# Two moves in the written-out order of a decoder trunk: the last tile's gate transposes, and one strip's low parts

## The reference

```python
for i in range(DEPTH):                                   # 2
    h = rms_norm(x, norm_mix_pre[i])
    proj = h @ w_in[i]                                   # 1024 x 2944
    y_a = gmlp_mixer(...)                                # 4 heads
    y_b = retention_mixer(...)                           # 6 heads
    y_c = swa_sink_mixer(...)                            # 6 heads, window 128, softmax with sinks
    mix = jnp.concatenate([y_a, y_b, y_c], axis=-1) @ w_out[i]
    x = x + rms_norm(mix, norm_mix_post[i])
    h = rms_norm(x, norm_ffn_pre[i])
    gate, up = split_cols(h @ w_ffn_in[i], (D_FF, D_FF)) # 2816 each
    f = (jax.nn.silu(gate) * up) @ w_ffn_out[i]
    x = x + rms_norm(f, norm_ffn_post[i])
    ple = rms_norm(p[i] @ w_ple_proj[i], ple_norm[i])    # 256 -> 1024
    x = x + jax.nn.sigmoid(x @ w_ple_gate[i]) * ple      # 1024 -> 1024
```

## Time and profile before

| | |
|---|---|
| median of 3 runs | 1223.09 us (1222.53 to 1223.4) |
| the profiled execution | 1222.93 us |
| its span, first to last instruction | 1221.2 us |
| TensorE busy | 1213.1 us, 7753 matmuls |
| VectorE, ScalarE, GpSimd busy | 843.1, 620.3, 175.6 us |
| mean granted TensorE clock | 1.000 |
| DMA | 126.36 MB, mean 103 GB/s |

### The profile page before, as it was taken

How to read it: one execution, slowest core, us unless ns; L and a number is a source line. 1 busy time by engine, 2 the same in 40 slices (tenths; PEclk the granted TensorE clock), 3 DMA queues, 4 the chain that set the end, 5 groups by cost and what they waited for, 6 DMA issues and landing times.

```text
span 1221.2 us, 20253 instructions
## 1 busy us (share of the span) xinstructions
PE 1213.1 (99%) x7753; PEld 1094.4 (90%) x7753; DVE 843.1 (69%) x1321; ACT 620.3 (51%) x1218; POOL 175.6 (14%) x260
## 2 busy tenths in 40 slices
PE   9999999999999999999999999999999999999998
PEld 7887988999999988888898879889999999888887
DVE  5665646888888843367977656468988887433788
ACT  7544426455555533347674643364655555322474
POOL 3044621000000000013030547120000000000120
PEclk9999999999999999999999999999999999999999
DMA  8332232233333354310344222331333333534001
GB/s 294 109 112 66 70 104 71 69 106 106 108 107 109 108 173 156 128 62 18 104 140 119 73 83 69 94 96 53 107 105 109 107 99 116 164 146 172 18 18 69
DMA packets 129135, 126.36 MB, mean 103 GB/s; under 512 B 5840, under 2 KB 111440, under 8 KB 129040
## 3 DMA queue, kind: packets, MB, share of 16 engines
q1 hardware_dynamic: 128352, 124.55, 32.7%
q10 hardware_dynamic: 688, 0.53, 0.2%
HBM read 120.99 MB, written 2.10 MB: 101 GB/s over the span
## 4 chain that ended last, share of the span: by engine, by line
PE 95%; DVE 3%; ACT 2%; issue 1%; POOL 0%; DVEq 0%; ACTq 0%
PE bank L1044 30%; PE bank L1046 29%; PE bank L1045 29%; PE bank L1275 2%; DVE w_lo L1978 1%; ACT prob L1739 1%; PE bank L1392 1%; PE bank L1332 1%; PE bank L1353 1%; PE bank L1376 1%; PE bank L1340 0%; PE bank L1388 0%; PE bank L1397 0%; DVE prob L2353 0%; PE bank L1285 0%
## 5 line engine op out<-in xcount | busy, mean ns | idle before, releaser
L1044 PE MATMUL bank<-h_hi,w_hi 128*128 128x256 f32 (+2 forms) x672 | 200.6, 298 | 0.1
L1046 PE MATMUL bank<-h_hi,w_lo 128*128 128x256 f32 (+2 forms) x672 | 199.9, 298 | 0.0
L1045 PE MATMUL bank<-h_lo,w_hi 128*128 128x256 f32 (+2 forms) x672 | 199.9, 297 | 0.0
L1976 DVE TENSOR_TENSOR w_lo<-raw,w_hi 128x1024 fp32r<-128x1024 f32 x70 | 83.2, 1226 | 133.7 <-ACT w_hi L1470 133.4
L1044 PE MATMUL bank<-w_hi,h_hi 128*128 128x384 f32 (+2 forms) x436 | 156.9, 360 | 0.8 <-DVE w_lo L1978 0.7
L1470 ACT ACTIVATE w_hi<-raw 128x1024 fp32r<-128x1024 f32 x70 | 70.6, 1053 | 160.6 <-PE bank L1046 160.6
L1045 PE MATMUL bank<-w_lo,h_hi 128*128 128x384 f32 (+2 forms) x436 | 151.8, 348 | 0.0
L1046 PE MATMUL bank<-w_hi,mid_lo 128*128 128x512 f32 x352 | 137.0, 389 | 0.0
L1044 PEld LDWEIGHTS bank<-h_hi,w_hi 128*128 128x128 f32 x672 | 128.6, 191 | 4.1 <-issue 0.5
L1046 PEld LDWEIGHTS bank<-h_hi,w_lo 128*128 128x128 f32 x672 | 128.6, 191 | 3.5
L1045 PEld LDWEIGHTS bank<-h_lo,w_hi 128*128 128x128 f32 x672 | 128.6, 191 | 3.4
(11 more groups left out here) (293 smaller groups left out, 2918.1 us busy)
## 6 DMA issues: line engine op xcount, KB each, us to landing
raw<-in_w_ffn_in SPq DMA_DIRECT2D x88, 512.0 KB, 3.8
raw<-in_w_ffn_out SPq DMA_DIRECT2D x44, 512.0 KB, 4.3
raw<-in_w_in SPq DMA_DIRECT2D x22, 512.0 KB, 5.3
raw<-in_w_in SPq DMA_DIRECT2D x24, 384.0 KB, 3.4
raw<-in_w_out SPq DMA_DIRECT2D x16, 512.0 KB, 3.8
gw<-in_w_gate SPq DMA_DIRECT2D x16, 512.0 KB, 3.7
raw<-in_w_ple SPq DMA_DIRECT2D x4, 512.0 KB, 5.9
x<-in_x_in SPq DMA_DIRECT2D x3, 512.0 KB, 6.9
```

The source lines that it names most:

```text
L1044: pe.matmul(out_ap, a_hi, b_hi, start=start, stop=False, skip_group_check=True)
L1045: pe.matmul(out_ap, a_hi, b_lo, start=False, stop=False, skip_group_check=True)
L1046: return pe.matmul(out_ap, a_lo, b_hi, start=False, stop=stop, skip_group_check=True)
L1976: last = dve.tensor_tensor(lo, raw[q % RAWS][:, cols], hi, ALU.subtract)
```

## The change

Two edits in `plan_schedule`, both in each of the two layers. After strip `("in", "bk", 1)` the one entry `conv` of strip a0 becomes two, `hi` at the same place and `lo` behind the entries of the next unit. And the entry `("T", "gate", 3)` moves behind `("mm", ple, 2)`.

```diff
     for layer in range(depth):
         at = plan_mixers()
         u = 4
+        late = None
         for s in ins[1:]:
             for m in range(TILES):
                 if u >= 6:
                     mm(s, m)
                 for e in at.pop(u, ()):
                     add(*e)
+                if late is not None:
+                    add("lo", late)
+                    late = None
                 u += 1
-            close(s)
+            if s == ("in", "bk", 1):
+                late = SIDX[s] + SLOTS
+                add("hi", late)
+            else:
+                close(s)
         mm(o[0], 0)
...
         mm(ple, 1)
         add("post", "ple", 0)
+        mm(ple, 2)
         add("T", "gate", 3)
-        mm(ple, 2)
         add("gsum", "S1")
         add("post", "ple", 1)
         add("gsum", "S3")
```

## The result

The changed kernel takes 1228.36 us (median of 5 runs, 1227.69 to 1228.58), the kernel before 1222.69 us beside it (5 runs, 1222.53 to 1223.4): 1.0044 times as long, interval 1.0033 to 1.0054. Forecast were 1226.4 us. The direction was right and the size was not: +5.7 us against +3.5, and 0.8 us above the upper end of the range.

A forecast was written before the change was run, and what follows sets the result against it. TensorE was taken to bound the kernel. From 1222.93 us, moving a0's low parts gave −2.0 us and moving the transposes 2 × 2.73 = +5.5, so 1226.4 us; the range was 1224.1 to 1227.6.

The forecast's parts named there:

- What bounds the kernel: Whole span: TensorE, busy 1213.1 of 1221.2 us, sets the time; moved instructions count only by changing its standstills.
- the start and ScalarE's side: Softmax of tile 2: swa_prev starts about 82.65, 3.7 us earlier; ScalarE's exponentials about 86.9, 2.1 us earlier.
- The spare 1.1 us: Softmax transposes: prob ready at 91.5, 1.1 us before TensorE wants it, covering a w_lo a quarter slower.
- signs of being wrong: Listed: a remaining wait for prob, a gate product under 2.5 us later, GpSimd's tile 1 addition at 0.2 us.
- the rule named in the prediction: VectorE and GpSimd: whichever takes the shared pair first holds it all instruction; applied to GpSimd's small addition, deciding 1.06 us.
- two pieces: Around side-projection tile 3: the 2.73 us per layer shows as TensorE waits, about 2.1 on h_lo, 1.0 on ple_n.
- (e): Side-projection tile 3: the new waits lower TensorE's clock, at most 1.7 us more a layer, 1229.8 us; chance 0.02.
- the second wait: Before the first gate product: TensorE waits 1.0 us for ple_n instead of 0.5.
- (a): GpSimd's small addition before ple_n starts first in both layers, moved transposes cost 1.67 us a layer: 1224.2 us; chance 0.08.
- (b): Later in the layer, short TensorE stops give back at most 0.5 us a layer: 1225.4 us; chance 0.06.
- (c): First gate product does not hang on the moved transposes; ple_n comes early, the 0.5 stop goes: 1219.9 us; chance 0.03.
- (d): Moving w_lo gains nothing, as beside GpSimd's rotations it ends over 1.1 us later than reckoned: 1228.4 us; chance 0.05.

The follow-up runs named there:

- low_only: Kernel before with only the low parts of strip a0 moved behind swa_prev, transposes left in place: 1222.64 us, 0.9997 of the kernel before.
- low_hold: Kernel before with a0's low parts moved, and GpSimd's rotation of tile 2 held until prob of that tile is normalised: 1220.66 us, 0.9981.
- hold_only: Kernel before with neither move, only GpSimd's rotation of tile 2 held until prob of that tile is normalised: 1223.65 us, 1.0005.
- trans_fill: Kernel before with only the transposes moved, plus eight unread matmuls behind them filling TensorE's stop: 1228.47 us, 1.0045.
- trans_post: Kernel before with the transposes moved, and side-projection tile 1's norm ahead of their copies and sum S1 on ScalarE and VectorE: 1227.27 us, 1.0037.
- trans_only: Kernel before with only the transposes moved behind side-projection tile 3 of 4, a0's low parts left in place: 1228.56 us, 1.0045.
- full_hold: Changed kernel with GpSimd's rotation of tile 2 held until prob of that tile is normalised: 1226.22 us, 1.0029 of the kernel before.
- full_hold_fill: Changed kernel with GpSimd's rotation of tile 2 held and eight unread matmuls filling TensorE's stop behind the transposes: 1225.88 us, 1.0026 of the kernel before.

## Why the prediction was right and wrong

**What bounds the kernel: right.** Every microsecond of the change is a stop of TensorE or a slower step of it.

**Edit 1, the start and ScalarE's side: right** to 0.1 us. **The gain, and the step that failed.** It is the sentence "I take 1.0, since 1.1 us of spare time cover a `w_lo` that is a quarter slower", which rests on "the four run in 4.2 us as before". The term of the sum was −2.0 us, and −0.4 came. `prob` came 1.9 us later than worked out: 0.75 from the small instruction, 0.8 from `w_lo`, 0.3 from the second small one, the rest from the last. The spare 1.1 us would have covered `w_lo` alone, which was less than a quarter slower; with the small instructions 0.8 us were left over. The 4.2 us of before were no property of the instruction: alone the four take 2.73 us, and what stands above that came with GpSimd's work beside them, and was 1.5 us at one place and 2.3 at the other. I took the slowdown as a constant, moved the work to where GpSimd runs other operations, and priced the small instructions at their undisturbed 0.17. The working saw only `w_lo` exposed, not the small ones ahead of and behind it. A wait for `prob` that is still there was the first of its own signs of being wrong. Shown by `low_only` against `low_hold` (5.02 to 2.73, 0.93 to 0.17, and 2.0 us of time), with `hold_only` ruling out that the hold itself brings it. Here the rule named in the prediction (the Trainium skill, "SBUF — State Buffer", section "SBUF: two separate sides": where VectorE's instruction has two SBUF inputs, the first of the two engines holds the shared pair for its whole instruction) belonged to edit 1 more than to edit 2. The trace agrees: the small instruction started at 85.18, behind a rotation that had started at 85.08 for 1.00 us, and ended at 86.10, as that rotation did; the second small one ended at 91.94, with the rotation of 90.45. And `y_lo`, one of whose inputs is in PSUM, took 0.54 us beside that same rotation, as it does with GpSimd still (0.55 in `low_hold`).

**Edit 2: right.** 2.73 us per layer as a block, in two pieces of 2.0 and 0.85 us of idle time, or 2.2 and 1.0 counted by starts as the forecast's 2.1 and 1.0 are. `trans_fill` measures it by itself: +5.5 in the span. `trans_post` shows that the reuse of the banks accounts for 1.73. The other 1.0 hangs on the order of the queues; whether on ScalarE's, as the prediction says, or on S1 ahead of the norm is not separated.

**The clock: left out of the sum, and wrong by 0.58.** Rival (e) named it at up to 1.7 a layer with a chance of 0.02. The clock fell behind 6 of the 8 stops of 2.0 us in the traces (one of two in the changed kernel and in `trans_post`, both in `trans_only` and `full_hold`), and at none of the 4 places where the stop was filled. (e) had the mechanism: the slow tile cost 1.57 us, of which the second wait hid 1.0. So a fall costs 0.50 to 0.59 us at the gate product, and only the last layer's stays. The Trainium skill ("TensorE: Matmul & The Clock Gate", section "Why this matters for your kernels") warns of idle gaps between bursts of matmuls; the trace agrees in kind, with a granted clock of 0.72, averaged over 6 us, behind a stop of 2.0 us.

**The rivals.** (a) did not occur: the addition lost by the same hair in both orders. (b) named the place where time is given back, but it was not edit 2's 2.73, of which nothing came back; it was the first layer's clock loss. (c) did not occur. (d), edit 1 giving nothing, was in substance what happened, by the mechanism that it names (`w_lo` ended at 91.04, 1.6 us later than reckoned), and had a chance of 0.05. That its 1228.4 meets the median of 1228.36 so closely is luck, since the 0.4 that edit 1 did give and the 0.58 of the clock nearly cancel; with both the sum is 1222.93 − 0.4 + 5.5 + 0.6 = 1228.6, measured 1228.49. The argument against (d), "it was so before too", was the mistake in one line. Half the way from the forecast to (d), where the range was to end, is 1227.4 and not 1227.6; the result lies above both.

**What stays open.** Why the clock fell in one layer and not in the other of the same execution. Where between 0 and 0.6 us it lies in a median is not resolved either: the profiled pair gives 0.50 at the place itself, the medians of `full_hold` and `full_hold_fill` 0.34. It is open too whether moving S1 alone would have taken the second wait away.

## What to carry to other kernels

An instruction's duration read from a trace belongs to its place. Before moving work on VectorE, look at what GpSimd runs at the new place, price the small instructions of the chain too, and look for a GpSimd operation that can be held back: here that turned a change without effect into −2.2 us. A step moved behind another is paid in full where its buffer is the next one to be written; and a wait removed is a gain only if nothing else behind it has become late: here it was kept in the second layer and lost again in the first.

## What the runs showed of the hardware

- Four 128x512 operations of VectorE with two SBUF inputs took 2.73 us with GpSimd still, 4.21 and 4.22 beside one set of its operations, 5.01 and 5.02 beside another. One of 128x6 elements took 0.17 us, or 0.92 behind a GpSimd operation that had started 0.10 us before. One with an input in PSUM took 0.54 us beside GpSimd and 0.55 without.
- A stop of TensorE of 2.0 us was followed in 6 of 8 cases by some 3 us at 1.2 GHz, and in 0 of 4 where matmuls filled it. Matmuls of 128x512 then started every 0.43 us instead of 0.23.
- That loss is not additive: in the first layers of `trans_only` and `full_hold` two short stops some 30 us later vanished, and the loss was given back by the next layer's transposes (608.45 against 608.42 us, 607.32 against 607.29).
